# The last four experts of a mixture-of-experts step are summed straight into the tokens, and the stored results come back as three entries of the weight stream

## The reference, cut to what matters

```python
def _moe(h, w_router, b_router, w_gu, b_gu, w_dn, b_dn):
    logits = h @ w_router + b_router
    top_v, top_e = lax.top_k(logits, TOP_K)          # 4 of 32 experts for each token
    gate = jax.nn.softmax(top_v, axis=-1)
    ...                                              # each expert e gets its own tokens xe:
        gu = xe @ w_gu[e] + b_gu[e]                  # 1024 -> 2048
        gt, up = jnp.split(gu, 2, axis=-1)
        gt = jnp.minimum(gt, 7.0); up = jnp.clip(up, -7.0, 7.0)
        act = gt * jax.nn.sigmoid(1.702 * gt) * (up + 1.0)
        out = act @ w_dn[e] + b_dn[e]                # 1024 -> 1024
    ...                                              # y[token] = sum over its 4 experts of gate * out
y = _rmsnorm(x + y, norm_final)
```

## Time and profile before

| what | value |
|---|---|
| three timed runs | 1376.31 us (1375.62 to 1378.55) |
| profiled execution, device time | 1378.33 us |
| its span | 1376.6 us |
| PE busy | 1278.2 us (93%) |
| DVE, ACT, POOL busy | 451.6, 240.0, 118.0 us |
| moved by DMA | 480.64 MB, mean 349 GB/s |
| mean granted PE clock | 0.991 |

### The profile page before, as it was taken

One profiled execution on the slowest core, in us unless ns is written; L12 is line 12 of the kernel. 1 busy time (PEld: TensorE's weight loads), 2 busy tenths in 40 slices (PEclk: granted clock), 3 DMA queues, 4 the chain that ended last, 5 costly groups with the idle time before them and its releaser, 6 DMA issues.

```text
span 1376.6 us, 14521 instructions
## 1 busy us (share of the span) xinstructions
PE 1278.2 (93%) x5975; PEld 579.7 (42%) x5975; DVE 451.6 (33%) x800; ACT 240.0 (17%) x345; POOL 118.0 (9%) x152
## 2 busy tenths in 40 slices
PE   7999999999999999999999999999988778787886
PEld 5756776766463333333333333333322222232231
DVE  1898312211254332222222224222332222233325
ACT  4112433310112121111111111111111111111112
POOL 1110100000001010101000000101001100000020
PEclk9999999999989999999999999999999999999998
DMA  9614634362779999999999999999999999999994
GB/s 332 247 62 178 229 122 182 124 245 98 268 292 399 428 424 426 425 427 426 425 426 427 426 426 426 426 426 423 426 426 426 425 426 425 425 426 425 425 393 152
DMA packets 64661, 480.64 MB, mean 349 GB/s; under 512 B 10937, under 2 KB 13113, under 8 KB 39865
## 3 DMA queue, kind: packets, MB, share of 16 engines
q1 hardware_dynamic: 51903, 460.67, 81.0%
q0 software_dynamic: 10672, 15.39, 3.2%
q10 hardware_dynamic: 1994, 3.25, 0.7%
HBM read 478.52 MB, written 22.61 MB: 364 GB/s over the span
## 4 chain that ended last, share of the span: by engine, by line
PE 67%; DMA 29%; DVE 1%; ACT 1%; issue 1%; SPq 1%; POOL 0%; DVEq 0%; ACTq 0%
PE PS L1751 26%; PE PS L1384 14%; DMA ring<-in_w_gu 13%; PE PS L1784 12%; DMA ring<-in_w_dn 10%; PE PS L1330 4%; PE PS L1574 4%; PE PS L1617 3%; DMA ring<-y_rows 3%; DMA arena<-in_w_dn 2%; PE PS L1413 2%; DMA arena<-in_mem_prompt 1%; PE PS L1660 1%; SPq L361 0%; PE PS L1522 0%
## 5 line engine op out<-in xcount | busy, mean ns | idle before, releaser
L1751 PE MATMUL PS<-ring,arena 128*64 128x512 f32 x1824 | 407.3, 599 | 36.5 <-DMA ring<-in_w_gu 29.3
L1241 DVE TENSOR_TENSOR arena<-PS,XX 128x1024 f32<-128x1024 f32 x32 | 39.2, 1225 | 658.8 <-PE PS L1751 658.8
L1751 PEld LDWEIGHTS PS<-ring,arena 128*64 128x64 f32 x1824 | 128.3, 139 | 293.7 <-issue 292.3
L1784 PE MATMUL PS<-ring,arena 128*64 128x512 f32 x896 | 202.5, 600 | 18.6 <-DMA ring<-in_w_dn 17.8
L1384 PE MATMUL PS<-arena,ring 128*128 128x320 f32 x768 | 213.2, 434 | 1.0 <-ACT arena L625 1.0
L1384 PEld LDWEIGHTS PS<-arena,ring 128*128 128x128 f32 x768 | 144.2, 190 | 60.0 <-issue 2.0
L1751 PE MATMUL PS<-arena 128*64 128x512 f32 x608 | 136.2, 595 | 14.4 <-DMA arena<-in_w_gu 13.9
L857 ACT ACTIVATE arena<-arena 128x1024 f32<-128x1024 f32 x32 | 33.9, 1058 | 617.6 <-DVE arena L1244 617.6
L539 POOL DMA_INDIRECT y_rows<-arena x60 | 59.7, 994 | 789.5 <-ACT arena L838 754.0
L1784 PEld LDWEIGHTS PS<-ring,arena 128*64 128x64 f32 x896 | 62.5, 137 | 142.1 <-issue 141.0
L1330 PEld LDWEIGHTS PS<-ident,arena 128*128 128x128 f32 (+4 forms) x596 | 64.3, 141 | 55.7 <-issue 47.9
(11 more groups left out here) (206 smaller groups left out, 685.9 us busy)
## 6 DMA issues: line engine op xcount, KB each, us to landing
ring<-in_w_gu SPq DMA_DIRECT2D x96, 2048.0 KB, 27.7
ring<-in_w_dn SPq DMA_DIRECT2D x48, 2048.0 KB, 28.9
arena<-in_w_gu SPq DMA_DIRECT2D x31, 2048.0 KB, 28.1
arena<-in_w_dn SPq DMA_DIRECT2D x16, 2048.0 KB, 30.4
ring<-in_w_in SPq DMA_DIRECT2D x11, 2048.0 KB, 12.7
ring<-in_w_mem_kv SPq DMA_DIRECT2D x2, 2048.0 KB, 20.1
ring<-in_cache_mem_k SPq DMA_DIRECT2D x4, 1024.0 KB, 12.4
ring<-in_cache_mem_v SPq DMA_DIRECT2D x4, 1024.0 KB, 14.3
```

Source lines behind the costliest of these rows:

```text
L1241: nc.vector.tensor_tensor(gbuf[:], PS[:, 0:2, :], g_bias, ALU.add).then_inc(main["g_added"], 1)
L1751: last = mm(PS[64 * h:64 * h + 64, 2 * g + b, :], in_block(xT[:, k, :], b), (spare[kk] if m == BONUS else moe_ring(m, 2)[:, kk]) [:, g * D ...
L1784: last = mm(PS[64 * h:64 * h + 64, 4 + b, :], actT[:, b, j, c * BLK:(c + 1) * BLK], moe_ring(m, 4)[:, j, h * 512:(h + 1) * 512], start=c = ...
```

## The change

`DIRECT` holds the last four experts, 28 to 31. Their results are no longer scattered. PE turns the one-hot matrix of each (`turn_hot`) and multiplies it with the result rows (`to_tokens`) between later chunks (`amid`, `last_experts`), into PSUM that DVE reads after each expert and each tile: DVE multiplies by the gate and adds to X (`add_tokens`). The gate is no longer in the matrix. `to_tokens` skips the second block when the expert has at most 64 tokens. The bias sums are added by DVE as a first triple of their own, during expert 29.

`y_rows` is stored by token, the four ranks of a token side by side: 16 KB in a row. Three entries (32, tt) are put into `STREAM` behind (30,3), and SP issues them like weight chunks: 2 MB, 2 MB and 1 MB. DVE adds them behind the activations of expert 30 (`add_ranks`). All of `y_rows` is zeroed now (5.2 MB in place of 2.6 MB). PE has no data-dependent jump over hundreds of instructions left ahead of the last matmuls; DVE has its own between the sums of expert 30 and those of expert 31.

```diff
+DIRECT = range(NE - 4, NE)
+_at = STREAM.index((NE - 2, 3)) + 1
+STREAM[_at:_at] = [(NE, tt) for tt in range(TT)]
...
-DIRECT = (NE - 2, NE - 1)
-RANK_PLACES = [PLACE[-10], PLACE[-9], PLACE[-6], PLACE[-5]]
...
 def consumed(m):
 
     e, c = STREAM[m]
+    if e == NE:
+        return "ranked", 0, TOPK * (c + 1)
...
             if CHUNKS[n] == "gB0":
                 sp.wait_ge(consts, 4)
-                sp.dma_start(y_rows[2 * T:4 * T, :].rearrange("(p j) c -> p (j c)", p=P).rearrange("p (n c) -> p n c", c=512),
-                             W[0].rearrange("p b t -> p (b t)")[:, None, 0:512].to_broadcast([P, 10, 512])) \
+                sp.dma_start(y_rows.rearrange("(p j) c -> p (j c)", p=P).rearrange("p (n c) -> p n c", c=512),
+                             W[0].rearrange("p b t -> p (b t)")[:, None, 0:512].to_broadcast([P, 20, 512])) \
...
+        def rank_rows(tt):
+            sp.dma_start(yr(tt)[0:ROWS[tt]], y_tokens[tt * P:tt * P + ROWS[tt]]).then_inc(yr_in[tt], 16)
+
         for i in range(RING, len(RINGED)):
-            free(0, RINGED[before_it(i)])
-            expert_chunk(RINGED[i]).then_inc(moe_loaded(RINGED[i]), 16)
+            m = RINGED[i]
+            free(0, RINGED[before_it(0, i)])
+            if is_rank(m):
+                sp.wait_ge(main["scattered"], 32 * DIRECT[0])
+                rank_rows(STREAM[m][1])
+            else:
+                expert_chunk(m).then_inc(moe_loaded(m), 16)
...
-        sp.wait_ge(main["dn_done"], NE - 2)
+        sp.wait_ge(main["gu_done"], NE)
         sp.dma_start(normfin, a["norm_final"].partition_broadcast(P)).then_inc(fin_in, 16)
...
-        rank_rows(0)
-        pool.wait_ge(main["scattered"], 32 * DIRECT[0])
-        rank_rows(1)
-        pool.wait_ge(main[consumed(RINGED[-6])[0]], consumed(RINGED[-6])[2])
-        rank_rows(2)
-        pool.wait_ge(main["gu_done"], NE)
-        rank_rows(3)
...
+        def add_tokens(t, signal):
+            for tt in range(TT):
+                r = ROWS[tt]
+                dve.wait_ge(main["tokens_done"], TT * (t - DIRECT[0] + 1) + tt + 1)
...
+                for x, sums in parts:
+                    if t in DIRECT:
+                        last = nc.vector.scalar_tensor_tensor(x, sums, GD[0:r, tt, 0, t:t + 1], x, ALU.mult, ALU.add)
+                    else:
+                        last = nc.vector.tensor_tensor(x, sums, x, ALU.add)
+                last.then_inc(signal, 1)
...
+                if v == 0 and e == DIRECT[3]:
+                    one_hot(NE - 1)
+                    add_tokens(DIRECT[1], main["summed"])
                 dve.wait_ge(main["spread_ready"], n)
                 dve.wait_ge(main["gu_done"], n)
...
+                if v == 0 and e == DIRECT[2]:
+                    for tt in range(TT):
+                        add_ranks(tt, 0, None)
...
+        add_tokens(NE - 2, main["summed"])
         with dve.If(most > WIN):
+            add_tokens(NE - 1, main["summed"])
             over_window(1)
...
+        with dve.Else():
+            add_tokens(NE - 1, tile_ready)
             dve.nop()
         dve.nop()
...
+        def to_tokens(t, tt):
+            r = ROWS[tt]
+            count = slots_used(0, t)
+            rows = ubuf if t == NE - 1 else Zs
...
+            with pe.If(count > BLK):
+                products(0, False)
+                products(1, True).then_inc(main["tokens_done"], 1)
+            with pe.Else():
+                products(0, True).then_inc(main["tokens_done"], 1)
...
+        def amid(e):
+            t = e - 2
+
+            def pieces(c):
+                if e == DIRECT[0] and c == 0:
+                    turn_gates()
+                if e == DIRECT[1] and c:
+                    bias_sum(c - 1)
+                if e - 1 in DIRECT and c == 0:
+                    turn_hot(e - 1)
+                if t in DIRECT and c:
+                    if c == 1:
+                        pe.wait_ge(w_copied, t - DIRECT[0] + 1)
+                        pe.wait_ge(main["zs_ready"], t + 1)
+                    else:
+                        sums_read(t - DIRECT[0] + 2, c - 2)
+                    to_tokens(t, c - 1)
+                if e == NE - 1 and c == 2:
+                    turn_hot(e)
...
+                    if v == 0 and e >= DIRECT[1]:
+                        sums_read(e - DIRECT[0], TT - 1)
                     down(v, e - 1)
...
+        def last_experts():
+            t = NE - 2
             pe.wait_ge(main["gu_read"], NE)
-            bias_sum(0, False)
-            bias_sum(1, False)
-            turn_act(0, NE - 1)
...
+            pe.wait_ge(main["zs_ready"], NE - 1)
+            to_tokens(t, 0)
+            to_tokens(t, 1)
             pe.wait_ge(main["actT_ready"], NE)
-            pe.wait_ge(main["zs_ready"], NE - 1)
-            down(0, e, amid_last)
-            to_tokens(0, 1)
-            to_tokens(0, 2)
+            down(0, NE - 1)
+            to_tokens(t, 2)
             pe.wait_ge(main["zs_ready"], NE)
             for tt in range(TT):
-                to_tokens(1, tt).then_inc(bd_done, 1)
+                sums_read(4, tt)
+                to_tokens(NE - 1, tt)
```

312 lines of the change are left out of this document (160 added, 152 removed).

## The result

The changed kernel takes 1389.96 us (median of 6 runs, 1387.43 to 1393.92), the kernel before beside it 1378.53. The ratio is 1.0082, with a 95% interval of 1.0063 to 1.0101: 11.4 us slower. The forecast was 1377.8 with a range to 1381.5, so the time lies outside it.

The account below looks back on a forecast made before the run. The weight stream on DMA was taken as the bound until the last chunks, then the wait for ranks; 1365.7 - 1364.5 - 0.3 = +0.9, plus 0.6, gave +1.5 on 1376.31: 1377.8 us, range 1373.2 to 1381.5.

Parts of the forecast that it names:

- D: End of PE's last weight chunk, (31,5): forecast at 1361.1 us, 4.8 later than before.
- A: Start of DVE's sum of expert 31 for the first tile: 1364.54 us before, forecast at 1365.7.
- The stream: Weight loads behind (30,3): 5.24 MB of ranks take 12.3 us at 426 GB/s, then the same 10 chunks, 49.2 us.
- The third rival: Rank loads in the weight stream: DVE's sums release chunks too late, or loads wait for scatters; 1381 and up, chance 0.06.
- PE at the end: Last eight chunks: PE becomes the bound, ending at 1361.1 where data would have allowed 1357.9.
- the half clock: PE's slower clock after idling 2.5 us at 1340: priced at 0, upper bound 1.7 us.
- The wait for DVE's sum and the restart: PE ahead of `down` of expert 30: 1.38 us for DVE's third-tile sum plus 1.1 for PE's restart.
- The jump: DVE's branch over further windows' code, between sums of experts 30 and 31: 3.5 us, bounds 2.4 and 6.6.
- the rival at full price: DVE's last branch costs 5.6 to 6.6 us as under load; total 1379.9 to 1380.9, chance 0.28.
- After A: From expert 31's first sum to the last store's issue: about 8.4 us, 0.3 less than before.
- The scatter, the zeroing, the sums of the ranks: Waits for expert 27's scatters, 2.6 MB more zeroing, DVE's twelve rank sums: all hidden, cost 0.
- allowance of 0.6 for restarts: Half of the 1.2 us by which PE's restarts ahead of two further `to_tokens` may show at the end.

Follow-up runs that it names:

- pairs in memory: Changed kernel with the third tile's ranks stored in pairs in `y_rows`, so one plain load of 128 rows fills 128 partitions: 1380.56 us, ratio 1.0014.
- the halves: Loads split into halves of 64 partitions: all rank loads of the changed kernel, 1402.32 us; eight weight chunks of the kernel before, 1419.95 us.
- the first tries on 128 partitions: Changed kernel, third tile's ranks into 128 partitions by one DMA with two-level source: 1408.37 us; also with expert 30's sums in both arms of DVE's branch: 1400.20.

## Why the prediction was wrong, point by point

All durations from the profiled executions, us; the third column is the run with the pairs in memory, which is the changed kernel without the slow load.

| step | forecast | changed | pairs in memory |
|---|---|---|---|
| (30,3) lands | 1292.6 | 1296.3 | 1292.6 |
| (29,4) behind it | 17.2 | 25.3 | 17.2 |
| (31,0) starts to D | 41.0 | 43.7 | 41.9 |
| D to A | 4.6 | 4.0 | 4.1 |
| A to the issue of the last output | 8.4 | 9.3 | 9.4 |

**The stream.** This step failed. It read "5.24 MB of ranks, 12.3 us", at the 426 GB/s of the weights. The loads took 20.4 us (25.3 less the 4.9 of the chunk), since one of the three goes into 64 partitions, and such a load takes the rate of all loads under way down to about half while two or more DMA engines are in it. The third rival named a broken stream, by DVE's sums or the scatter, with 0.06; that did not happen. Its time (1381 and up) was of the right side for a wrong reason. The trace of before had the sign, a rate of 385 GB/s with a DMA share of 1.00, and packets of weights of 0.79 to 0.92 us beside loads of 64 rows:

```profile
1320.00:1340.00 20.00, 14.93 (x71) 5.12 (x69) 8.04 (x8) 1.49 (x2) 3.74 (x6) 1.00 1.02 385
```

I had averaged over 1260 to 1310 and over the end and not looked at the stretch between.

The Trainium skill, page "SBUF — State Buffer", section "Door 1: The DMA port swizzle (why `[64,N]` ≈ `[32,N]`)", states that partitions 0 to 63 reach 8 of the 16 ports on which DMA writes, and so half the rate. The 215 to 231 GB/s of the halves against 427 agree. The Trainium skill, page "DMA: Bandwidth & Descriptors", section "Back-pressure in remote DMA", says for writes to another core that a saturated port holds up other engines on the same path; that weights slowed down with the ranks would fit, but no run here shows the ports, nor why one engine alone in such a load slows nothing.

**PE at the end.** The direction was right: PE and not data bounds the end, D comes 8.2 us after the last landing (1354.1) in the run with the pairs, and the forecast had 7.0. In the changed kernel 1.7 us more come from the half clock, 8.78 for 7.09, which I had named and priced at 0: a second term that failed. Twelve traces have this idle time, 2.60 to 2.70 us; in ten of them the half clock came behind it, in two, the run with the pairs and one of the first tries on 128 partitions, it did not. What decides it stays open.

**The wait for DVE's sum and the restart.** Forecast 2.5 us, measured 2.70 and 2.61. Right. With other work for PE there, 1.7 us of it and the half clock behind it were gone.

**The jump.** Forecast 3.5 us between the end of PE's products of expert 30 for the third tile (D + 1.1) and A, so A = D + 4.6; measured D + 4.0. The branch and the first instruction behind it stand 2.9 us apart in the changed kernel (1376.54 to 1379.44), and 6.6 in the kernel before (1332.16 to 1338.76); the rival at full price (0.28) did not come.

**After A.** Forecast 0.3 less, measured 0.6 more: DVE stands 1.10 us between the first and second sum. This term had the wrong sign. The idle time goes when the branch moves ahead of the sums of expert 30, so it belongs to the branch; why the jump costs a second time, behind the first instruction that it lands on, is not shown. I had booked 1.3 us for the jump ahead of A and nothing behind it; it was 0.8 ahead and some 1.3 behind.

**The scatter, the zeroing, the sums of the ranks.** As forecast at nothing: the zeroing landed 22.0 us after its issue, 8 us before the next DMA was issued; the loads were issued with 40 us of queue ahead; and the twelve sums ended at 1325.1, while the first DMA engine came to (30,5), which waits for the last of them, at 1336.3.

The sum: 0.9 of the forecast (its allowance of 0.6 for restarts did not show beside these steps), 8.1 of the stream, 2.7 of PE, -0.6 of the jump and 0.9 behind A are 12.0. With the 3.1 us from the start of the kernel and the 0.6 by which (30,3) came later still, 15.7 against the 15.6 between the two profiled executions. Without the 64-partition load, 1380.56 against 1378.11 is +2.4 us (ratio 1.0014, so +0.4 to +3.3), and the forecast of +1.5 lies in it.
